# One stage for the differential projection, the latent and the differential attention of the second model

## What is computed

```python
h = rms_norm_2(x, mix_norm)
z = h @ w_in
c_q, c_kv, k_rope_raw, dq, dk, dv, gate_mla, gate_diff = jnp.split(z, cuts, axis=-1)
y_mla  = mla_branch(c_q, c_kv, k_rope_raw, ...)    # latent attention: 8 heads, q and k of 96, v of 64
y_diff = diff_branch(dq, dk, dv, ...)              # differential: 4 heads, two softmaxes of 64 each, v of 128
merged = sigmoid(gate_mla) * (y_mla @ w_proj_mla) + sigmoid(gate_diff) * (y_diff @ w_proj_diff)
x = x + merged @ w_out

# differential attention, per head, causal:
a = causal_probs(q1, k1) - lam * causal_probs(q2, k2)
out = rms_norm_2(a @ v, subln) * (1.0 - lam_init)
```

## Time and profile before

| | |
|---|---|
| median of three runs | 3459.44 us (3458.34 to 3470.52) |
| the profiled execution, its own time | 3446.28 us |
| its span in the trace | 3444.5 us |
| mean granted clock of TensorE | 0.927 of full speed |
| PE busy | 3019.9 us (88%) |
| DVE busy | 968.0 us (28%) |
| ScalarE busy | 703.7 us (20%) |
| POOL busy | 402.5 us (12%) |
| 16 DMA engines, first queue | 42.2% of the span |

### The profile page before, as it was taken

The page is one execution under the profiler, slowest core; times in us unless marked ns, Lnnn a source line. Parts: engine busy times, 40 slices in busy tenths (PEclk is TensorE's granted clock), DMA queues, the critical chain, the costliest instruction groups (busy, mean ns, idle before and its releaser), DMA issues.

```text
span 3444.5 us, 48553 instructions
## 1 busy us (share of the span) xinstructions
PE 3019.9 (88%) x21001; PEld 1832.4 (53%) x21001; DVE 968.0 (28%) x1752; ACT 703.7 (20%) x1352; POOL 402.5 (12%) x552
## 2 busy tenths in 40 slices
PE   6998979599999798885877775999989988989998
PEld 2444535345544344543433333887854667658876
DVE  2024733311111214524000003223241472232232
ACT  2013631000000213520000003222220551122231
POOL 1013420122221111401111110000000000000000
PEclk9998989799999898897999997999999699999999
DMA  9910033799999600036999996222121102212230
GB/s 354 354 62 0 1 134 117 277 402 404 404 406 406 233 25 1 0 140 267 409 413 410 411 414 239 98 74 98 66 79 50 56 1 74 73 55 98 74 132 27
DMA packets 141016, 631.97 MB, mean 183 GB/s; under 512 B 12848, under 2 KB 20032, under 8 KB 85520
## 3 DMA queue, kind: packets, MB, share of 16 engines
q1 hardware_dynamic: 122064, 577.67, 42.2%
q0 software_dynamic: 18752, 51.29, 4.8%
HBM read 605.79 MB, written 23.13 MB: 183 GB/s over the span
## 4 chain that ended last, share of the span: by engine, by line
PE 72%; DMA 15%; DVE 7%; ACT 3%; issue 3%; SPq 0%; POOL 0%; DVEq 0%; ACTq 0%; POOLq 0%
PE bank L783 38%; DMA slots<-in_w_up_dram 12%; PE bank L1130 8%; PE bank L1222 7%; PE bank L1139 3%; PE bank L1151 3%; PE bank L982 2%; PE bank L961 2%; PE bank L1314 1%; PE bank L1158 1%; PE bank L796 1%; DMA arena<-in_ada_w_dram 1%; PE bank L1323 1%; DVE small L2155 1%; DVE arena L2196 1%
## 5 line engine op out<-in xcount | busy, mean ns | idle before, releaser
L1130 PE MATMUL bank<-slots,HT 128*32 128x256 f32 x8192 | 499.2, 395 | 104.8 <-DMA slots<-in_w_gate_dram 62.4
L1130 PEld LDWEIGHTS bank<-slots,HT 128*32 128x32 f32 x8192 | 274.3, 114 | 329.0 <-issue 83.7
L783 PE MATMUL bank<-slots,HT 128*128 128x512 f32 (+2 forms) x960 | 405.3, 582 | 23.5 <-ACT done_mark L1917 17.7
L783 PEld LDWEIGHTS bank<-slots,HT 128*128 128x128 f32 x960 | 183.4, 193 | 231.4 <-issue 210.2
L783 PE MATMUL bank<-hT_high,chunk_high 128*128 128x512 f32 x704 | 277.5, 394 | 8.5 <-DVE low_slots L2421 8.5
L783 PE MATMUL bank<-hT_high,low_slots 128*128 128x512 f32 x704 | 277.9, 395 | 0.0
L783 PE MATMUL bank<-hT_low,chunk_high 128*128 128x512 f32 x704 | 277.0, 393 | 0.0
L2332 DVE TENSOR_TENSOR arena<-bank,arena 128x512 f32<-128x512 f32 x32 | 22.1, 691 | 677.2 <-ACT arena L1680 677.2
L783 PE MATMUL bank<-HT,slots 128*128 128x512 f32 (+1 forms) x480 | 180.3, 532 | 8.2 <-ACT done_mark L1917 5.4
L1680 ACT ACTIVATE arena<-bank 128x512 f32<-128x512 f32 x32 | 19.1, 598 | 773.4 <-PE bank L1130 444.5
L783 PEld LDWEIGHTS bank<-hT_high,chunk_high 128*128 128x128 f32 x704 | 132.9, 189 | 38.8 <-issue 9.2
(11 more groups left out here) (373 smaller groups left out, 4044.3 us busy)
## 6 DMA issues: line engine op xcount, KB each, us to landing
slots<-in_w_gate_dram SPq DMA_DIRECT2D x128, 1024.0 KB, 21.3
slots<-in_w_up_dram SPq DMA_DIRECT2D x128, 1024.0 KB, 23.8
arena<-in_w_down_dram SPq DMA_DIRECT2D x64, 1024.0 KB, 23.4
arena<-in_ada_w_dram SPq DMA_DIRECT2D x48, 1024.0 KB, 8.5
X<-in_w_down_dram SPq DMA_DIRECT2D x48, 1024.0 KB, 26.9
slots<-in_w_in_dram SPq DMA_DIRECT2D x15, 2048.0 KB, 12.8
slots<-in_ffn_w_gate_dram SPq DMA_DIRECT2D x10, 2048.0 KB, 8.0
slots<-in_ffn_w_up_dram SPq DMA_DIRECT2D x10, 2048.0 KB, 8.6
```

Source lines behind the costliest of these rows:

```text
L783: mm = pe.matmul(out_, lhsT, rhs, start=(n == 0), stop=(n == len(pairs) - 1))
L1130: mm = pe.matmul(bank[32 * j:32 * j + 32, 2 + n, 256 * g:256 * g + 256], xT[:, 64 * k + 32 * g:64 * k + 32 * g + 32], columns(w[:, c, :], ...
```

## The change

The stage diff_in is gone; its work is spread over the first 40 steps of attend_two. The order of units becomes 24 latent ones (query tiles 0 to 2), the 32 differential ones, and the last 8 latent ones. In step s PE now issues `scores(s)`, two or three of the 96 projection matmuls, `turn_probs(s-2)`, `mix(s-3)` and the transposes due, so the lead grows by a step. probs2 and probs2T have three buffers instead of two. The banks are handed out by a plan:

| bank | steps 0 to 39 | after |
|---|---|---|
| 0, 1 | projection of q, k | scores (0), transposed probabilities (1) |
| 2 | projection of v | sums of even pairs |
| 3 | transposes of q, k and y | the same |
| 4, 5 | scores, in turn | scores, in turn with 0 |
| 6 | transposed probabilities | the same, in turn with 1 |
| 7 | sums of all pairs | sums of odd pairs |

The copy of transposed probabilities is on ScalarE only for differential units with s = 0, else on DVE. DVE copies and rotates q and k of token tile i at the end of step 10i+7, in a single buffer that takes the place of gain_row; the gain is therefore loaded in merge. The roots of a differential tile that begins at pair f are taken in step 2f+12, its normalising is in step 2f+13. At the end the loop runs to 70 steps instead of 74.

```diff
-    return diff + latent
+    return latent[:-L_HEADS] + diff + latent[-L_HEADS:]
+PROJECT_STEPS = 40
+class PlanTwo:
+    def __init__(self):
+        self.units = units_two()
+        n = len(self.units)
+        self.uses = [ST, 0, ST, 0, 0, 0, 0, 0]
+        self.scores = [self.use((4 + p % 2) if p < PROJECT_STEPS else (4, 5, 0)[(p - PROJECT_STEPS) % 3]) for p in range(n)]
+        self.turned = [self.use(6 if p < PROJECT_STEPS or p % 2 else 1) for p in range(n)]
+        self.sums = [self.use(7 if g < PROJECT_STEPS // 2 or g % 2 else 2) for g in range(n // 2)]
...
+        self.steps = n + 6
+        per = PROJECT_STEPS // ST
+        self.rows_step = [per * i + 7 for i in range(ST)]
+        self.values_step = [per * i + per for i in range(ST)]
+        turns = [(per * i + 9 + n, ("q", "k")[n], i) for i in range(ST) for n in range(2)]
+        for g in range(n // 2):
+            kind, tile = self.units[2 * g][:2]
+            first = self.first_pair[tile]
+            turns.append((2 * first + 15 + g - first if kind else 2 * g + 6, "y", g))
...
+    def projections(self, step):
+        per = 3 * KD * ST
+        if step >= PROJECT_STEPS:
+            return []
+        return [(m // (3 * KD), m // KD % 3, m % KD)
+                for m in range(per * step // PROJECT_STEPS, per * (step + 1) // PROJECT_STEPS)]
+    def finished_tile(self, step):
+        return self.first_pair.index(step // 2) if step >= 0 and step % 2 == 0 and step // 2 in self.first_pair else None
+    def probs_on_act(self, p):
+        return self.units[p][0] == 1 and self.units[p][3] == 0
...
-        probs2 = spare[:, 0:2 * SEQ].rearrange("p (a n) -> p a n", a=2)
-        probs2T = spare[:, 2 * SEQ:4 * SEQ].rearrange("p (a n) -> p a n", a=2)
+        probs2 = [spare_rows[:, 0, :, :], spare_rows[:, 1, :, :], HT[:, 0:4, SEQ + P:NTOK]]
+        probs2T = [spare_rows[:, 2, :, :], spare_rows[:, 3, :, :], HT[:, 4:8, SEQ + P:NTOK]]
...
PE:
+                def mix(p):
+                    kind, qt, h, s = units[p]
+                    (from_, read), (b, use) = plan.turned[p], plan.sums[p // 2]
+                    pe.wait_ge(sem[f"free{from_}"], at_bank(st, from_, read))
+                    if s == 0:
+                        pe_may_fill(pe, st, b, use)
...
+                for step_ in range(plan.steps):
+                    if step_ < n:
+                        scores(step_)
+                    for part in plan.projections(step_):
+                        project_part(*part)
+                    if 2 <= step_ < n + 2:
+                        turn_probs(step_ - 2)
+                    if 3 <= step_ < n + 3:
+                        mix(step_ - 3)
+                    for event in plan.turns_of(step_):
+                        turn(*event)
...
ScalarE:
+                for step_ in range(plan.steps):
+                    if step_ < n:
+                        exponentials(step_)
+                    if 2 <= step_ < n + 2 and plan.probs_on_act(step_ - 2):
+                        take_probs(step_ - 2)
+                    if step_ in plan.values_step:
+                        take_values(plan.values_step.index(step_))
+                    if step_ % 2 == 0 and first <= (step_ - 6) // 2 < last:
+                        squares((step_ - 6) // 2)
+                    if plan.finished_tile(step_ - 12) is not None:
+                        roots(plan.finished_tile(step_ - 12))
+                    for event in plan.turns_of(step_):
+                        take_turned(*event)
...
DVE:
+                for step_ in range(plan.steps):
+                    if step_ < n:
+                        maximum(step_)
+                    if 2 <= step_ < n + 2 and not plan.probs_on_act(step_ - 2):
+                        take_probs(step_ - 2)
+                    if plan.finished_tile(step_ - 13) is not None:
+                        normed(plan.finished_tile(step_ - 13))
+                    if step_ % 2 and 0 <= (step_ - 5) // 2 < n // 2:
+                        rows_of_y((step_ - 5) // 2)
+                    if step_ in plan.rows_step:
+                        rows_of_qk(plan.rows_step.index(step_))
...
POOL:
-                name = {"ffn_up1": "mix_norm_2", "latent_in0": "ffn2_norm_2", "ffn_up2": "final_norm_2"}[f"{st.name}{st.layer}"]
+                name = {"ffn_up1": "mix_norm_2", "merge0": "ffn2_norm_2", "ffn_up2": "final_norm_2"}[f"{st.name}{st.layer}"]
```

More of the change, by code:

```diff
@@ new lines, with use, turns_of @@
+PROJECT_STEPS = 40
[7 more added lines that the diff above has]
+        self.sums = [self.use(7 if g < PROJECT_STEPS // 2 or g % 2 else 2) for g in range(n // 2)]
+        self.first_pair = [[self.units[2 * g][:2] for g in range(n // 2)].index((1, tile)) for tile in range(ST)]
+        self.steps = n + 6
[7 more added lines that the diff above has]
+            turns.append((2 * first + 15 + g - first if kind else 2 * g + 6, "y", g))
+        turns.sort(key=lambda turn: turn[0])
+        self.turns = [(step, what, i, self.use(3)[1]) for step, what, i in turns]
+        self.turn_use = {(what, i): use for _, what, i, use in self.turns}
+    def use(self, b):
+        self.uses[b] += 1
+        return b, self.uses[b] - 1
+    def turns_of(self, step):
+        return [turn[1:] for turn in self.turns if turn[0] == step]
+    def projections(self, step):
[8 more added lines that the diff above has]
+        return self.units[p][0] == 1 and self.units[p][3] == 0
@@ L1344, in attend_two, with turn @@
-                for i in range(n + 10):
-                    if i < n:
-                        scores(i)
-                    if 1 <= i <= n:
-                        turn_probs(i - 1)
-                    if 2 <= i <= n + 1:
-                        mix(i - 2)
-                    for g in turned_at(i):
-                        turn_y(g)
+                def turn(what, i, use):
+                    if what == "y":
+                        pe.wait_ge(sem["y_rows"], st.at("y_rows", i + 1))
+                    else:
+                        pe.wait_ge(sem["qk_rows"], st.at("qk_rows", i + 1))
+                    pe_may_fill(pe, st, 3, use)
+                    if what == "y":
+                        mm = pe.transpose(bank[:, 3, 0:P], y_rows2[:, i % 8, :], ident[:, :])
+                    else:
+                        for c in range(4):
+                            mm = pe.transpose(bank[:, 3, tile_cols(c)], qk_diff[:, tile_cols(4 * (what == "k") + c)], ident[:, :])
+                    mm.then_inc(sem["full3"], 1)
@@ L1852, in roots, with take_turned @@
                                    scale=1.0 / (2 * HD)).then_inc(sem["y_root"], 1)
[L1854 to L1871 removed]
+                def take_turned(what, i, use):
+                    act.wait_ge(sem["full3"], at_bank(st, 3, use))
+                    if what == "y":
+                        kind, qt, h, _ = units[2 * i]
+                        chunk = h // 2 if kind == 0 else 4 + h
+                        act.activation(yT[:, chunk, tile_cols(qt)], bank[:, 3, 0:P], ACT.Copy).then_inc(sem["free3"], 1)
+                    else:
+                        dst = q_diffT if what == "q" else k_diffT
+                        act.activation(dst[:, :, tile_cols(i)], bank[:, 3, :].rearrange("p (h n) -> p h n", h=4), ACT.Copy)\
+                            .then_inc(sem["free3"], 1)
@@ L2543, in rows_of_y, with take_probs @@
+                def take_probs(p):
+                    qt, (b, use) = units[p][1], plan.turned[p]
+                    dve.wait_ge(sem[f"full{b}"], at_bank(st, b, use))
+                    dve.tensor_copy(probs2T[p % 3][:, 0:qt + 1, :], bank[:, b, 0:qt * P + P].rearrange("p (c n) -> p c n", n=P))\
+                        .then_inc(sem[f"free{b}"], 1)
                 def rows_of_y(g):
                     kind = units[2 * g][0]
-                    b = 4 + g % 2
+                    b, use = plan.sums[g]
```

238 lines of the change are left out of this document (89 added, 149 removed).

## The result

The changed kernel takes 3492.59 us (median of 4 runs, 3489.38 to 3493.83), the kernel before 3464.55 us (4 runs, 3458.34 to 3470.52). The ratio is 1.0064, with a 95% interval of 1.0047 to 1.0082. The forecast was 3451 with a range up to 3468, and its chance for a kernel slower by more than 0.5% was 0.09.

The account below looks back on a forecast made before the run. The 236.1 us of projection and attention were taken as bound by TensorE, partly at 1.2 GHz. Work 193.2, bank waits 27.4, weights 2, roots 3 and drain 2 made 227.6, so 3451 us for the kernel, range 3431 to 3468.

Parts of the forecast that it names:

- the first term of the sum: TensorE's whole work in projections and attention at full clock: 193.2 us, of it 107.3 for the units, against 236.1 now.
- the low 56 us of before: Time inside the differential units of the kernel before with the granted clock at 0.50 while TensorE shows as busy.
- The waits for bank 7: Steps 5 to 41: the mix waits for VectorE to free the sums' single bank, 19 times, 27.4 us.
- the 2 us for work behind them: After each wait for bank 7 TensorE loads the mix's weights uncovered, about 0.1 us each, 2 us in all.
- the banks of scores and transposes: Banks 4, 5 and 6 until step 40: no cost, since 0.86 us projections, twice or three times, stand between uses.
- The roots: Square roots of differential tiles on ScalarE, with two table loads: TensorE waits 3 us in all, bounds 0 and 8.5.
- the Trainium skill's figure for a table load: 2.66 us a switch with its drain on ScalarE; would add some 4 us to the roots.
- Projections, POOL, SP, and what follows: VectorE's work beneath projections, moved gain DMA, SP's queue: no cost; merge or later stages change by at most 3 us.
- 227.6: Forecast time in us of the merged projection and attention stage, against 236.1 before, 8.5 less.
- The clock: Rival: 19 gaps in the merged stage hold the clock low; at 56 us low, 20 us slower, 3479; chance 0.18.
- the expert window: Evidence against the clock rival: a window in the experts with TensorE busy 69% keeps clock 1.00.
- The Trainium skill's rule: Small idle gaps, repeated as banks are cycled, make the clock swing between two levels; by it the clock rival is likeliest.

Follow-up runs that it names:

- e1: Changed kernel, but VectorE does rows_of_y before take_probs while projections last; 3445.69 us, ratio 0.9971 to the kernel before, stage 221.1 us.
- e11: e1 with projections over 48 steps instead of 40 and the normalising of finished tiles behind the bank's freeing; 3421.86 us, ratio 0.9896 to the kernel before.
- e13: Changed kernel with differential scores over 128 rows instead of 64 (does not compute the layer); stage 232.2 us against 263.1.
- e8: e1 with the turn of the keys one step later; 3452.85 us, ratio 0.9941 to the kernel before, stage 216.4 us.
- e10: e8 with differential scores over 128 rows instead of 64 (does not compute the layer); stage 199.2 us.
- e14: Kernel before the change with differential scores over 128 rows instead of 64; attention units 131.5 us against 148.8.
- e7: e1 with the 64-row score product of the last two differential tiles made three times; stage 252.8 us.
- e12: e7 with the extra score products over 128 rows, the used ones left at 64; stage 234.6 us.

## Why the prediction was wrong

**The failed step is the first term of the sum: PE's work at the full clock, 107.3 us for the units, with the low 56 us of before counted as won.** Nothing in the trace had shown why the clock was low there; that projections between the units would lift it was assumed. They do go with a full clock where they stand beside 64-row products and no gap past the first unit's is over 0.9 us (e1 up to step 40, e11 up to step 48), not where longer gaps come with them, nor in the third tile once they end. The low time stayed (61.4 us for 64.9), which costs 28.2 us of the stage. What the runs showed in place of the assumption is that each low piece begins at a gap and that 64-row scores prolong it: with the gaps kept and 128 rows it is 10.2 us (e13), with 64 rows and the main gaps gone 30.7 (e1).

**The waits for bank 7 were right**, one by one: 27.0 us in 19 for 27.4 in 19, the longest 3.0 us in step 37, the last at 2788. The cause given, DVE's order, is shown by e1_order. Its count is not quite the same thing as the profile's: it had the 0.16 us by which the mix starts later than unhindered inside the price, where the profile counts idle time alone. What goes with the waits, in e1_order, is 24.5 us of idle time and 3.4 more; so the 2 us for work behind them were short by some 1.5 us.

**A missed term: bank 3**, 5.9 us. Keys, queries and y are turned through it one at a time, and in step 40 a turn of y stands right behind that of the keys, 2.2 us. The prediction listed the banks of scores and transposes as covered and did not look at this one.

**The roots** were put at 3 us; only 0.4 us of waits for ScalarE's probabilities is left. That is partly luck: PE, slowed by the clock and by the changes of rows, comes late enough. In e13, where it is quicker by both, such waits come to 4.4 us. By the Trainium skill's figure for a table load (page "ScalarE: Activation LUTs", section "What ACT_TABLE_LOAD costs") an estimated 4 us would have been added; no wait of the changed kernel shows this.

**Projections, POOL, SP, and what follows** cost nothing, as said: the rest of the kernel differs by 1 us.

Together: 227.6 + 28.2 (clock) + 5.9 (bank 3) - 2.6 (roots) = 259.1 us for the 262.8 from the first matmul to the end of the stage. Some 1.5 of the 3.7 us left are the work behind the waits; the rest is not assigned. With the clock largely restored, in e13, the stage came to 232.2 us, 4.6 above the sum, but through errors that cancel: its units are also cheaper by the 12.6 us of the changes of rows, which the distances of the earlier trace rows hold.

**The rivals.** "The clock" was right in place, kind and nearly in size: 56 us low, 28 lost, 20 slower than before; measured 61, 28 and 27 for the stage, the rest being mostly bank 3. Its reason, the gaps, was right for the start of each low piece; most of the length hangs on the 64 rows. Its chance of 0.18 was too low: the earlier trace rows, the expert window that kept the full clock in spite of its gaps, weighed against it, but that window has no 64-row product. The Trainium skill's rule named with it, small gaps again and again making the clock swing (page "TensorE: Matmul & The Clock Gate", section "A second HAM failure mode: psum-queue depth-cycling"), is borne out in part: 31 us of low time went with 24.5 us of waits in e1_order, but with the gaps kept and 128 rows only 10 us are low.

## What to carry to other kernels

Time that a kernel spends at the low clock is no gain until a run shows what brings the clock back: look for the wait that stands where the clock falls, and find out what keeps it low by changing one property of the work, such as the rows of a product, at the same instruction count. Where a bank is single, the engine that frees it should do so before anything that waits for PE's newest work, and each single bank needs its own line in the sum. A "busy" PE can hide both few rows and a stop between products of different rows, so compare the distances from start to start of whole units, not durations.

## What the runs showed of the hardware

Scores over 64 of 128 rows cost this kernel twice: 0.39 to 0.41 us each time that the rows change to 64 and back (e8 against e10), and a granted clock that, once a wait of 1.6 to 2.2 us had dropped it, stayed at 1.2 GHz for 27 to 58 us while PE shows busy above 90%. Over 128 rows single low pieces lasted 3 to 7 us, and a whole stage had 3 (e10), 10 (e13) and 20 (e14). Extra products of 64 rows lengthened the low stretch from 31 to 48 us (e7), as many of 128 rows cut it to two pieces of 3.4 (e12). At the low clock a unit lost 46% of its time. Whether rows of zeros would serve as well as rows of data, which might give these stages a correct kernel near the time of e10, was not tried, and why the low stretch ends after one tile in some runs and after almost two in others is open.
